# A new row table for the gathers of a hybrid attention, delta-net and PEER layer

## The reference, cut to what matters

```python
q = (ht @ w_q).reshape(t, PEER_HEADS, PEER_QDIM)
s1 = jnp.einsum('thd,hkd->thk', q[..., :PEER_HALF], sub_keys_1)   # s2 likewise
v1, i1 = lax.top_k(s1, PEER_TOPK)
cand = (v1[..., :, None] + v2[..., None, :]).reshape(t, PEER_HEADS, PEER_TOPK * PEER_TOPK)
best, ci = lax.top_k(cand, PEER_TOPK)
experts = e1 * N_KEYS + e2                     # 8 heads x 16 experts for each token
gates = jax.nn.softmax(best, axis=-1)
u = u_table[eb]
act = jax.nn.gelu(jnp.einsum('thkd,td->thk', u, xb)) * gb
vv = v_table[eb]
out = jnp.einsum('thk,thkd->td', act, vv)
```

## Time and profile before

| what | us |
|---|---|
| median of 3 runs | 3694.66 |
| lowest and highest run | 3689.73, 3706.08 |
| the profiled execution | 3676.49 |
| its span | 3674.5 |
| busy in the span: PE, DVE, POOL | 2450.8, 2333.9, 2303.8 |

### The profile page before, as it was taken

The page is one execution under the profiler, slowest core; times in us unless marked ns, Lnnn a source line. Parts: engine busy times, 40 slices in busy tenths (PEclk is TensorE's granted clock), DMA queues, the critical chain, the costliest instruction groups (busy, mean ns, idle before and its releaser), DMA issues.

```text
span 3674.5 us, 44635 instructions
## 1 busy us (share of the span) xinstructions
PE 2450.8 (67%) x15137; PEld 1389.0 (38%) x15137; DVE 2333.9 (64%) x5605; ACT 869.4 (24%) x2454; POOL 2303.8 (63%) x2091
## 2 busy tenths in 40 slices
PE   7686656857568587578568577578658753444466
PEld 6565524644244255343144155344234310111122
DVE  4538987866866877566866777666777575444300
ACT  4323212322113133232123133223113210111111
POOL 0004775655666777666766767666776677666665
PEclk9898777978788689788589789789778875555589
DMA  7725998999899999999999999999999999999998
GB/s 239 257 78 172 348 328 296 400 352 327 318 338 361 352 399 413 402 345 352 358 350 373 351 352 413 384 375 365 365 347 384 351 340 361 370 364 364 361 367 324
DMA packets 389011, 1258.29 MB, mean 342 GB/s; under 512 B 43630, under 2 KB 92851, under 8 KB 380595
## 3 DMA queue, kind: packets, MB, share of 16 engines
q0 software_dynamic: 294912, 1073.87, 78.1%
q1 hardware_dynamic: 75442, 139.62, 10.4%
q10 hardware_dynamic: 18432, 41.95, 3.2%
HBM read 1217.50 MB, written 37.78 MB: 342 GB/s over the span
## 4 chain that ended last, share of the span: by engine, by line
PE 26%; DVE 26%; issue 15%; POOL 13%; DMA 7%; another core or an unknown queue 5%; ACT 3%; DVEq 3%; ACTq 1%; SPq 0%; POOLq 0%
PE zz L1614 12%; DVE u_ring L1163 10%; PE va L1614 8%; POOL u_ring L732 7%; POOL v_ring L749 6%; DMA v_ring<-in_peer_v,idxT 3%; DMA u_ring<-in_peer_u,idx 3%; PE rr L1614 3%; PE ox L1614 2%; DVE work L1379 1%; DVE work L1220 1%; PE rr L1618 1%; DVE work L1361 1%; DVE work L1444 1%
## 5 line engine op out<-in xcount | busy, mean ns | idle before, releaser
L732 POOL DMA_INDIRECT u_ring<-in_peer_u,idx x1024 | 1193.4, 1165 | 824.0 <-issue 286.8
L749 POOL DMA_INDIRECT v_ring<-in_peer_v,idxT x960 | 1041.3, 1085 | 499.5 <-issue 252.7
L1614 PE MATMUL va<-v_ring,column 128*32 128x256 f32 x7680 | 828.0, 488 | 566.3 <-DMA v_ring<-in_peer_v,idxT 328.9
L1163 DVE SCALAR_TENSOR_TENSOR u_ring<-u_ring,hn_t 128x1024 f32<-128x1024 f32 x896 | 1058.8, 1221 | 110.9 <-DMA u_ring<-in_peer_u,idx 82.2
L1614 PE MATMUL zz<-work 128*128 128x256 f32 (+3 forms) x2880 | 667.1, 393 | 109.6 <-issue 48.8
L1614 PEld LDWEIGHTS va<-v_ring,column 128*32 128x32 f32 x7680 | 259.6, 126 | 1098.1 <-issue 520.9
L1614 PEld LDWEIGHTS zz<-work 128*128 128x128 f32 (+1 forms) x2880 | 490.7, 212 | 310.2 <-issue 194.4
L813 ACT ACTIVATE column<-onehot,wT 128x32 f32<-128x32 f32 x1024 | 277.0, 314 | 919.2 <-remote 442.8
L1163 DVE SCALAR_TENSOR_TENSOR u_ring<-u_ring,zz 128x1024 f32<-128x1024 f32 x128 | 155.6, 1220 | 193.2 <-DMA u_ring<-in_peer_u,idx 173.3
L1614 PE MATMUL rr<-work,later 128*128 128x512 f32 x144 | 101.2, 807 | 68.2 <-DVE work L1364 35.7
L1570 DVE TENSOR_TENSOR y_buf<-va,y_buf 128x1024 f32<-128x1024 f32 x8 | 9.8, 1219 | 207.4 <-PE va L1614 201.5
(11 more groups left out here) (315 smaller groups left out, 2773.7 us busy)
## 6 DMA issues: line engine op xcount, KB each, us to landing
work<-d_w SPq DMA_DIRECT2D x42, 1024.0 KB
work<-in_w_out ACTq DMA_DIRECT2D x64, 512.0 KB
u_ring<-in_peer_u,idx POOLq DMA_INDIRECT x1024
v_ring<-in_peer_v,idxT POOLq DMA_INDIRECT x960
work<-d_kT SPq DMA_DIRECT2D x36, 256.0 KB
work<-d_v SPq DMA_DIRECT2D x36, 256.0 KB
w_q_t<-in_peer_w_q SPq DMA_DIRECT2D x1, 8192.0 KB, 24.1
w_q_t<-in_w_in SPq DMA_DIRECT2D x7, 1024.0 KB
```

The source lines that it names most:

```text
L732: g.indirect_dma_start(u_ring[:, n % RU, :], None, u_rows, bass.IndirectOffsetOnAxis(idx[b % 2][:, s:s + 1], 0)).then_inc(u_landed[n % RU] ...
L749: g.indirect_dma_start(v_row(n), None, v_rows, bass.IndirectOffsetOnAxis(idxT[b % 3][:, t:t + 1], 0)).then_inc(v_landed[slot] if slot < RV ...
L1163: v.scalar_tensor_tensor(u_ring[:, m % RU, :], u_ring[:, m % RU, :], 1.0, token, ALU.mult, ALU.mult, accum_out=dots[:, s:s + 1]).then_inc( ...
L1614: return t_.matmul(out_, lhsT, rhs, start=start, stop=stop, skip_group_check=True)
```

## The change

The dictionary of weights is replaced by two, one for U and one for V rows, and each point has a weight for three kinds of block: block 1, even blocks, odd blocks from 3 on. The projection's points get ten weights, one for each four points, in place of four. The marks of `PACE` are new, and so is `FIRST`. The functions that use them stay as they are.

```diff
--- before.py
+++ after.py
@@ -128,30 +128,39 @@
     return any(0 <= m < NCH and needs_tokens(m) for m in (n - 7, n - 8))
 
 
-SHARES = {"start": ((6, 6, 6), (7.2, 6, 6)),
-          "level": ((6, 6, 5.9, 6, 6), (6, 6, 6, 6, 8.2)),
-          "state": ((7, 7), (7, 9.8)),
-          "key": ((9, 9, 9), (9, 9, 9)),
-          "mix": ((7.1,), (8,)),
-          "out": ((10.8, 10), (7, 10)),
-          "hn": ((8,), (9.3,)),
-          "pq": ((10, 9.8, 10, 10), (10, 15.9, 10, 10)),
-          "score": ((7.9,), (29.7,)),
-          "top": ((7, 7, 7, 8.5, 7), (7, 7, 7, 11, 7)),
-          "p": ((5, 7.1, 5, 2.5), (5, 5.3, 5, 2.5))}
+U_SHARES = {"start": ((7.5, 6, 14.3), (7.5, 13.2, 11), (7.5, 6, 11)),
+            "level": ((6.9, 7.8, 4.1, 6, 5.1), (6.9, 7.8, 5.9, 6, 10.1), (5.9, 6, 5.9, 11.2, 6)),
+            "state": ((3.4, 10.7), (3, 10.7), (2, 10.7)),
+            "key": ((10.4, 6.7, 6.4), (5.5, 11.7, 5.4), (6.5, 9.3, 10.1)),
+            "mix": ((3.2,), (2.7,), (0,)),
+            "out": ((17.3, 9.2), (38.1, 8.5), (10.8, 11.5)),
+            "hn": ((0,), (8.5,), (4.9,)),
+            "pq": ((19.4, 11.3, 22, 10), (13, 9.8, 0, 10), (2, 9.8, 10, 5.8)),
+            "score": ((3.7,), (7.9,), (10,)),
+            "top": ((3.6, 10.2, 6, 6.8, 7), (3.5, 10.2, 0, 8.5, 7), (7, 10.2, 7, 8.5, 7)),
+            "p": ((5, 7.1, 7.1, 7.1, 5, 8, 8, 2.5, 3.7, 2.3),)}
+V_SHARES = {"start": ((5.4, 8, 0), (8.3, 1.8, 2.4), (8.3, 6, 5.1)),
+            "level": ((6.2, 7.7, 3.6, 16.6, 4), (9.6, 0, 6, 14.4, 12.5), (9.6, 6.9, 6, 14.4, 8.2)),
+            "state": ((11.2, 24.8), (7.8, 3.4), (8, 8)),
+            "key": ((7.6, 9, 1.9), (7.6, 11.7, 7.2), (8.7, 9, 22)),
+            "mix": ((8,), (12.8,), (3.5,)),
+            "out": ((11.6, 0), (2, 6), (0, 7)),
+            "hn": ((8.1,), (0,), (4,)),
+            "pq": ((7.5, 3.1, 9.2, 7.2), (14.9, 15.6, 10, 11.1), (14.9, 0, 10, 11.1)),
+            "score": ((0,), (40,), (18.9,)),
+            "top": ((7.9, 1.6, 3.5, 0, 0), (7, 33.9, 3.9, 11, 7), (11.2, 8, 7, 11, 7)),
+            "p": ((3.5, 6.9, 5.3, 2.6, 3.5, 5, 4.7, 2.5, 2.2, 1.8),)}
 FREE_BANK = {"start": 0, "level": 0, "state": None, "key": 1, "mix": 1, "out": 1, "hn": None, "pq": 1, "score": 1, "top": 1}
 
 
-def shares(name, k, count):
-
-    u, v = SHARES[name]
+def shares(name, b, k, count):
+
+    of_block = 0 if name == "p" or b == 1 else 1 + b % 2
     if name == "key":
-        i = 0 if k == 0 else 2 if k == count - 1 else 1
+        k = 0 if k == 0 else 2 if k == count - 1 else 1
     elif name == "p":
-        i = 0 if k < 4 else 3 if k >= NCH else 1 if k < GV_END else 2
-    else:
-        i = k
-    return u[i], v[i]
+        k = k // 4
+    return U_SHARES[name][of_block][k], V_SHARES[name][of_block][k]
 
 
 def points():
@@ -160,16 +169,16 @@
     for b in range(1, NB):
         if segment_before(b) is not None:
             for n in range(NCH + 9):
-                yield ("p", segment_before(b), n), *shares("p", n, 0), None if n < 4 or token_turn_pending(n) else 1
+                yield ("p", segment_before(b), n), *shares("p", b, n, 0), None if n < 4 or token_turn_pending(n) else 1
         for name, count in (("start", 3), ("level", 5), ("state", 2), ("key", b + 1), ("mix", 1), ("out", 2), ("hn", 1),
                             ("pq", 4), ("score", 1), ("top", 5)):
             for k in range(count):
-                yield (name, b, k), *shares(name, k, count), FREE_BANK[name]
-
-
-
-PACE = {1: (128, 28), 2: (250, 118), 3: (341, 207), 4: (498, 366), 5: (593, 463), 6: (760, 626), 7: (884, 752)}
-FIRST = 0.60
+                yield (name, b, k), *shares(name, b, k, count), FREE_BANK[name]
+
+
+
+PACE = {1: (128, 29), 2: (256, 127), 3: (354, 214), 4: (510, 394), 5: (617, 493), 6: (766, 640), 7: (896, 758)}
+FIRST = 0.57
 
 
 def table():
```

## The result

The changed kernel takes 3726.54 us (median of 5 runs, 3691.16 to 3742.35) against 3694.66 (median of 5, 3689.73 to 3706.08). The ratio of the two sets of runs is 1.0074 with a 95% interval of 1.0038 to 1.0109 (the quotient of the two medians alone would be 1.0086): slower by 0.7%, where 3671 was forecast. The profiled execution took 3711.06 us, 34.6 more than that of before; its span is 3708.2 us, 33.7 more. All lines of the kernel lie nine further down: the dot is L1172, the U gather L741, the V gather L758, the matmul L1623, the wait for the output projection L1418.

The account below looks back on a forecast made before the run. DMA was taken as nearly full, the rest being small hold-ups of engines that free ring slots. Stretch terms, from -28 us (tail) to +28 us (block 5), summed to -24 us: 3694.7 to 3671, range 3628 to 3712.

Parts of the forecast that it names:

- block 2: Mixing of block 2: 14 added rows partly covered by 32 us of idle DMA, +5 us; some 234 us, share over 0.93.
- block 5: Mixing of block 5: 28 added rows, most of the idle not reached, +28 us; some 344 us long.
- third projection: Third projection stretch: 23 rows fewer at 0.87 us a row, -20 us; -32 if all DMA.
- tail: After block 7's last point: 19 rows fewer at 1.46 us, -28 us; 256 dot instructions, some 575 us long.
- -3 inside even blocks: Even blocks: U rows move to the first "out" point, where DVE waits for the output projection; -3 us for three blocks.
- POOL's waits for a dot: POOL's waits for a dot to free a U slot should fall from 254 us.
- the sign that was named for too large shares of "out": At the output projection: if DVE comes after PE, so that PE waits for h, the shares are too large.
- the overlap: Mixing blocks: idle DMA, 122 us in blocks 2 to 7, takes part of the added rows' transfers.
- rival (b): Whole kernel: DMA work conserved, idle only changes place, 1.40 us per moved row; -3 us, 3692; chance 0.22.
- The line set in the prediction: Prediction is wrong if blocks 2 to 5 together grow by over 60 us.
- (c): Idle DMA filled wherever rows come, stretches losing rows shrink at full price; -66 us, 3629; chance 0.15.
- (d): POOL's issue is the limit where DVE works, 1.46 us a row in block 5; +23 us, 3718; chance 0.13.

Follow-up runs that it names:

- n2: Rows of the kernel before, given out by the new form of the code, against the kernel before (3691.01 us, slow chip): ratio 0.9989.
- n1: The changed kernel run once more, against the kernel before (3691.01 us, slow chip): ratio 1.0095.
- c1: Rows of the kernel before, given out by the new form of the code, against the kernel before (3438.13 us, fast chip): ratio 0.9988.
- c2: The changed kernel run once more, against the kernel before (3438.13 us, fast chip): ratio 0.9971.
- m1: Old table with block 5's marks raised, 28 rows more there from the third projection and block 6, against the kernel before (3690.62 us): ratio 1.0018.
- m2: Old table with block 7's marks raised, 16 rows (12 U, 4 V) more there from the tail, against the kernel before (3690.62 us): ratio 1.0009.
- e7: Changed kernel with U and V weights of mix, out and hn evened out in even and odd blocks, against the kernel before (3439.54 us, fast chip): 1.0058.
- n3: Changed kernel with U and V weights of mix, out and hn evened out in even and odd blocks, against the kernel before (3691.01 us, slow chip): 1.0087.
- n4: Changed kernel with V marks of blocks 4, 5 and 6 taken back to 370, 478 and 626, against the kernel before (3691.01 us, slow chip): 1.0094.

## Why the prediction was wrong

**Its sum beside the chips.** The change of each stretch in us, new less old table, from where its last row was taken; A is before and after, E is n2 and n1, C is c1 and c2:

| stretch | rows | forecast | A | E | C |
|---|---|---|---|---|---|
| block 1 | +1 | 0 | +7.2 | +11.2 | -4.8 |
| first projection | 0 | 0 | -5.7 | -4.0 | -3.2 |
| block 2 | +14 | +5 | +8.2 | +9.1 | -2.4 |
| block 3 | +5 | +3 | +20.6 | +12.8 | +13.1 |
| second projection | -2 | -2 | -1.6 | -20.0 | -2.3 |
| block 4 | +8 | +4 | +15.0 | +20.0 | +4.2 |
| block 5 | +28 | +28 | +43.7 | +43.4 | +48.2 |
| third projection | -23 | -20 | -31.9 | -29.9 | -26.9 |
| block 6 | -14 | -12 | -7.4 | -16.2 | -22.6 |
| block 7 | +2 | +1 | +15.9 | +11.4 | +12.3 |
| tail | -19 | -28 | -30.4 | -24.5 | -25.9 |
| sum | 0 | -24 (with -3 inside even blocks) | +33.6 | +13.3 | -10.3 |

A single stretch of one profile is uncertain by 10 us and more: the second projection with the old rows took 216.2, 229.5, 222.4 and 225.8 us (A, E, m1, m2), block 3 286.6, 293.9, 286.8 and 282.6, block 6 321.9, 318.7 and 336.3 (A, E, m2).

**What was right.** The tail (256 dots, 573 us for the 575 named). The third projection gave back more than forecast, 32 us, the end that DMA alone sets (23 x 1.40). Block 2 was named at 234 us with a share over 0.93 and came to 237 with 0.95. (Block 5 was named at 344 and came to 361.) POOL's waits for a dot fell. DVE's wait for the output projection fell, and with it came the sign that was named for too large shares of "out": PE waits for DVE there. Evening the shares out (e7, n3) made no run faster all the same.

**The step that failed** is the overlap: that rows added to the mixing blocks are taken by idle DMA ("7 us against 14 idle: +3" for block 3, "11 against 18: +4" for block 4, "+1" for block 7, "+5" for block 2, 0 for block 1, "+28" for block 5). In these six stretches the sum has 58 rows more, 81 us of transfers at 1.40, for +41 us, so idle DMA was to take 40. Measured, in us:

| six stretches together | time | transfers | idle DMA |
|---|---|---|---|
| forecast | +41 | +81 | -40 |
| A | +110.6 | +94.5 | +18.3 |
| E | +107.9 | +92.9 | +17.2 |
| C | +70.6 | +86.4 | -14.4 |

(Transfers are the busy time of the 16 engines, idle is against a share of 1.02.) On the slow chips idle took none of the rows and grew; on C it took 14 us, all of it in blocks 1 and 2. The transfers came to 5 to 14 us more than the sum had. The gathers in flight at the bounds moved too: the old table ends blocks 4 and 6 with 11 to 14 gathers issued ahead, the new one with 5 to 7. So block 5's +28 was not bad by itself: m1 has +31, and of the +43.7 here some 10 come from block 4, whose own +4 was then nearer +25.

Over the whole run, from the first dot to the last V row, idle DMA went from 200.3 to 231.1 us on A (+30.8, the last row +33.6 later), from 199.4 to 217.2 on E (+17.8, +13.3), and from 69.2 to 58.4 on C (-10.8, -10.3), and the transfers stayed the same to within 5 us. That is rival (b)'s conserved work. It was right on the price of a row (m2: no gain from 16 rows out of the tail into block 7 that can be told) and wrong in taking the idle as fixed.

Block 2's idle fell by 14 us on A, 11 on E and 17 on C, so the gain forecast for it is real, and on the slow chips it is given back elsewhere. Where, the four profiles of old rows (A, E, m1, m2) and the two of new ones (A, E) tell for blocks 3 and 4, and for some 4 us in block 7: 13 to 22 us of idle became 27 and 28 in block 3, and 13 to 20 became 26 and 25 in block 4. In block 1 it was 34 to 39 us and became 45 and 44, but it is 35.7 and 34.5 in n3 and n4, which have the same rows there. In block 6 it was 14, 11 and 27 with the old rows, 28 and 16 with the new. On C no block gained more than 4.

The line set in the prediction, blocks 2 to 5 longer by over 60 us together, was passed: 87.5 on A. It was passed on C as well, with 63.1, where the time fell, so it was no sure sign.

**The rivals.** (c), 3629, is out on every chip. (d) gave 3718, near the 3726 measured, but not by its cause: it wanted POOL to be the limit in block 5, and there POOL is busy 248.74 of 361 us, the same 69% as before, with gathers at (121.84 + 126.89) / 222 = 1.12 us in place of 1.16; the total of 126.89 is that of the 113 V gathers. The Trainium skill (SBUF — State Buffer, Who interferes with whom) says that GpSimd reads and DVE instructions with two SBUF inputs contend. The distance of 1.12 to 0.94 us between block 5 and the tail agrees with it, but the tail has less DVE work of every kind, no run here takes the DVE work away from the same rows, and it did not set the time. The rate that the Trainium skill (DMA: Bandwidth & Descriptors, Anatomy of one DMA) states, 436e3 bytes per us, gives an estimate of 1.20 us for 512 KB; the tail shows 1.46 on A (603.0 / 413) and 1.31 on C (542.7 / 413).

**What is settled and what is not.** Shown: the sign goes with the chip, or with whatever made it slow or fast that time (1.0074 and 1.0095 where the kernel before takes 3691 to 3695, 0.9971 and 0.9980 where it takes 3438 to 3440); idle DMA did not take the added rows, but for block 2; on B the marks cost more than the weights, and on C V marks raised without U marks cost 1.0187; neither the burst nor the coinciding gate is the cause of the loss on E. The marks of blocks 5 and 7 alone measured 0.18% and 0.09%, neither of which can be told from zero. Open: which of the weights and marks bring the new idle of blocks 3 and 4 on a slow chip, and through which wait. The waits for V slots rose with it on A and E (108.9 to 188.3 us, 105.6 to 140.5) and not on C, but on B a run with 132.1 us of them and one with 174.8 took the same time, so they are not the cause by themselves. No version that was run on both kinds of chip beats the kernel before on both: the new table, with or without its gate apart, is the best on C and D, the old one on A, B, E and F.

## What to carry over

Where DMA work is conserved, the time is work plus idle, so ask of a new order which idle it takes away and which it makes. Idle that a stretch shows on average is not room for rows: of the 40 us that the sum let it take, it took none on the slow chips and 14 on the fast one. Where stretches are bounded by rows taken, count the gathers in flight at each bound too. A table tuned to fractions of a per cent is tuned to one chip: have the kernel before measured beside it on a second chip before a difference of 0.3 to 1% is believed. Where two streams are chained (V behind the weights of U), don't raise the marks of the second alone.

## What the runs showed of the hardware that was not expected

One and the same program takes 3438 us on one chip and 3695 on another, 7% apart, at nearly the same granted clock (0.780 in c1, 0.786 before). In the tail of the old table DMA moves 404 GB/s at a share of 1.03 on C, 366 at 0.98 on A. The queue of gathers has 80.4% of 3444.6 us on C, 1.352 us a row, against 1.401 on A:

```profile
q0 software_dynamic: 294912, 1073.87, 80.4%
```

So of the 230 us between the two spans the longer transfers of the gathers are 2048 x 0.049 = 100, and more idle DMA (200.3 against 69.2) the other 131. One trace of where it comes from: on A, POOL waits 137.8 us in 84 waits for something that the profile calls remote, before it may issue a V gather. On C its list of waits has no such row.

```profile
POOL v_ring L749 <- remote: 137.8, 84, 3.7
```

POOL also waits longer for dots on A, 254.3 us against 175.3. What "remote" is, and why the chips differ, no run here shows. Nor is it on record what else ran on a chip meanwhile, so another load beside the program is as open a cause as the chip itself.
